# A top-2 mixture of experts layer on one Trainium2 core: residual carried in each expert's rows, last expert added from SBUF

## The chip, the cores and the metric

The program runs on one core of one Trainium2 chip. The metric is the device time of one execution in microseconds (us); lower is better. Engines: PE (TensorE, matrix multiplication), DVE (VectorE), ACT (ScalarE), POOL (GpSimd) and SP (SyncE, which here only issues transfers). SBUF is the on-chip memory of 128 partitions, PSUM holds eight banks of 128x512 floats, into which PE writes.

## The reference

The input is 512 tokens of 1024 floats. A token mixer comes first (input projection, a gated linear recurrence and a short convolution, output projection), then a layer norm. What the change touches is the second half:

```python
alpha = 2 ** 0.25
# h: 512 x 1024, the first norm's output
# 32 experts in 4 groups; each token takes 2 experts of 1 group, with weights w
hid = silu(h @ w_gate[e]) * (h @ w_up[e])          # 1024 -> 256
ffn = sum over the token's 2 experts of w * (hid @ w_down[e])
out = layer_norm(alpha * h + ffn, ln2_g, ln2_b)
```

Each expert has 1 MiB (1,048,576 bytes) each of gate, up and down weights: 96 MiB for 32 experts, read once.

## The kernel before

**Up to the routing (0 to some 187 us).** PE computes the two projections in split float32 while DVE and ACT run the recurrence. Weights of the first experts are loaded as soon as their SBUF is free. Per tile of 128 tokens the first norm's rows `h1` are stored to DRAM (`h1_rows`, two half rows of 2 KB for each token) and the router's logits are taken. Then small matmuls with one-hot operands make two tables, `x_rows` and `y_rows`: for each expert a column of 128 row numbers (64 slots, two half rows each). `x_rows` says where a slot's token lies in `h1_rows`, `y_rows` where the result goes in `y_pairs`, a DRAM buffer of 2 x 512 tokens. Empty slots carry a number outside the buffer and move nothing. Experts with more than 64 tokens get overflow items; with the inputs here there are none.

**The loop over 32 experts.** The work is one list of instructions for each engine, in a fixed order; semaphores tie the lists together. For item q:

- POOL gathers the tokens' rows into `xg` (line 676) and later scatters the results from `ys` (line 681).
- PE, `pe_item`, line 1141: `turn_x(q + 1)` transposes the next item's rows (line 1092), `gate_up(q)` is 16 float32 matmuls (line 1102), `down(q - 1)` is 4 (line 1131), `turn_hid(q)` transposes the hidden values (line 1122). In item 2 there is also a small sum that makes the overflow tables (line 1059).
- DVE copies the transposed rows to SBUF (line 1469), makes `hid` (line 1541), copies it transposed (line 1546). ACT does the silu (line 841) and copies the result out of PSUM to `ys` (line 848).
- SP loads weights into a ring of 8 slots (`RING`). `refill_gu(q)` (line 555) waits for `gu_summed` of item q - 8, `refill_dn(q)` (line 559) for `dn_summed`. Down weights have a ninth slot (`wdn_once`), filled once at 175.96 us, so that those of expert 8 are there without a refill. SP's order is fixed too: a refill that waits holds up those behind it.

There are two row buffers for gathers and two for results (`ROWS = 2`). A gather waits until PE has transposed the buffer's earlier content (line 693), a scatter until ACT has copied the result (line 699).

**The end.** Behind the last weights SP loads `h1` back from DRAM (2 MiB, line 576). The scale and offset of the second norm (`ln2g`, `ln2b`) are asked for once the scatter of expert 28 has landed (line 588). After all scatters SP loads `y_pairs` as eight 512 KB pieces (line 599). PE adds, in PSUM, alpha * h1 by a scaled identity (line 1193) and both experts' rows by diagonal matrices of the routing weights (line 1200); DVE takes the statistics for each of four tiles (line 1585) and finishes the norm with ACT and POOL; SP stores.

Of the kernel before, what the change touches and what calls it, by code (L numbers as in the profile page):

```python
# [21 lines left out]
F32 = mybir.dt.float32  # L22
# [9 lines left out]
P = 128  # L32
# [3 lines left out]
ROWS = 2  # L36
# [11 lines left out]
PIECES = 4  # L48


def hybrid_moe_layer(
# [28 lines left out]
    with ExitStack() as ctx:  # L80
# [15 lines left out]
        ident = sb("ident", [P, P])  # L96
        tri = sb("tri", [P, P], BF16)
        ones = sb("ones", [P, P], BF16)
# [46 lines left out]
        up_block = iota_f[:, 120:120 + 1 + MAX_OVER]  # L145

# [13 lines left out]
        ys = [sb(f"ys{b}", [P, H]) for b in range(ROWS)]  # L160
        xg = [sb(f"xg{b}", [P, H]) for b in (1, 0)][::-1]
# [5 lines left out]
        place[0] = max(place[0], shared + 16384)  # L167
# [15 lines left out]
        wdn.append(at("wdn_once", [P, 2, D], F32, spare + 24576))  # L183
# [52 lines left out]
        iota_i = at("iota_i", [P, 140], I32, y_base + 4096)  # L236
# [7 lines left out]
        h1 = at("h1", [P, TT, D], F32, ring + SLOT)  # L244
        ln2g = at("ln2g", [P, D], F32, ring + SLOT + 16384)
        ln2b = at("ln2b", [P, D], F32, ring + SLOT + 20480)
        pair_y = [[at(f"pair_y{k}_{t}", [P, D], F32, ring + 2 * SLOT + 4096 * (TOP_K * t + k)) for k in range(TOP_K)] for t in range(TT)]


        diag = at("diag", [P, 1 + TOP_K * TT, P], F32, ring + 3 * SLOT + 8192)  # L250
# [6 lines left out]
        hot_slot = at("hot_slot", [P, NP, BLOCK], F16, shared + 4096)  # L257
        hot_x = at("hot_x", [P, NP, N_EXP], F16, shared + 5120)
        hot_y = at("hot_y", [P, NP, N_EXP], F16, shared + 5632)
# [4 lines left out]
        over_slot = at("over_slot", [P, NP, BLOCK], F16, wr_place)  # L264
        over_cmp = at("over_cmp", [1, MAX_OVER, N_EXP], F16, route + 3072)
        assert wr_place + NP * BLOCK * 2 <= wr_place + KT * NR * 4


        DVE_ADDED = 1
# [23 lines left out]
        dn_in = [sem(f"dn_in{s}") for s in range(RING + 1)]  # L293
# [57 lines left out]
        weights_ready = sem("weights_ready")  # L351
# [19 lines left out]
        pairs_in = [[sem(f"pairs_in{t}_{k}") for k in range(TOP_K)] for t in range(TT)]  # L371
        h1_in = sem("h1_in")
        diag_ready = sem("diag_ready")
# [41 lines left out]
        def in_order(rows):  # L415

            return rows.rearrange("p (a m j) -> p m a j", a=2, j=4)
# [28 lines left out]

        def dn_slot_of(q):
            return q if q < RING + 1 else (q - 1) % RING

        def dn_loads_of(q, r):  # L450

            return r + (1 if q < RING + 1 else (q - 1) // RING + 1)
# [42 lines left out]
        def _(sp_):  # L495
# [7 lines left out]

            for q in range(PIECES):
                load_x(q)
                load_first(q)
# [11 lines left out]

            def load_dn(e, s, done):
                sp_.dma_start(wdn[s][:, :, :].rearrange("p j d -> p (j d)"), dn_of(e)).then_inc(done, 16)  # L520
# [27 lines left out]
            load_dn(RING, RING, dn_in[RING])  # L548
# [10 lines left out]
            def refill_dn(q):  # L559
                sp_.wait_ge(dn_summed, q - RING + (0 if q <= 2 * RING else 1))  # L560
                load_dn(q, dn_slot_of(q), dn_in[dn_slot_of(q)])


            for q in range(RING, 2 * RING + 1):
                refill_gu(q)
                if q > RING:
                    refill_dn(q)
            refill_gu(2 * RING + 1)
            for q in range(2 * RING + 1, N_EXP):
                if q + 1 < N_EXP:  # L570
                    refill_gu(q + 1)
                refill_dn(q)

            last_of_1 = max(q for q in range(N_EXP) if slot_of(q) == 1)
            sp_.wait_ge(gu_summed, last_of_1 + 1)
            sp_.dma_start(h1[:, :, :].rearrange("p t (a h) -> p t a h", a=2),
                          h1_rows.rearrange("(t p a) h -> p t a h", p=P, a=2)).then_inc(h1_in, 16)
# [10 lines left out]
            sp_.wait_ge(y_scattered[(N_EXP - 4) % ROWS], 16 * ((N_EXP - 4) // ROWS + 1))  # L588
# [7 lines left out]
            for t in range(TT):  # L596
                for k in range(TOP_K):
                    src = y_pairs[2 * (k * T + t * P):2 * (k * T + (t + 1) * P), :]
                    sp_.dma_start(pair_y[t][k][:, :], src.rearrange("(p a) h -> p (a h)", a=2)).then_inc(pairs_in[t][k], 16)
            for t in range(TT - 1):  # L600

                sp_.wait_ge(out_ready_pool, t + 1)
                sp_.wait_ge(out_ready, t + 1)
                sp_.dma_start(out_rows[t * P:(t + 1) * P, :], pair_y[t][1][:, :]).then_inc(out_stored, 16)
            for h in range(2):

                sp_.wait_ge(out_ready, TT + h)
                cols = slice(h * H, (h + 1) * H)
                sp_.dma_start(out_rows[(TT - 1) * P:, cols], pair_y[TT - 1][1][:, cols]).then_inc(out_stored, 16)
# [4 lines left out]
        def _(pool):  # L614
# [15 lines left out]
            pool.iota(iota_i[:, 108:116], pattern=[[2 * P, TOP_K * TT]], base=-int(NO_ROW), channel_multiplier=2).then_inc(const_pool, 1)  # L630
            pool.memset(iota_i[:, 116:120], int(NO_ROW)).then_inc(const_pool, 1)
            pool.wait_ge(const_pool, 10)
# [3 lines left out]
            pool.wait_ge(const_pool, 11)  # L636
            pool.memset(iota_i[64:128, 116:117], int(NO_ROW) + 1).then_inc(const_pool, 1)
            pool.wait_ge(const_pool, 12)
            pool.memset(zeros[:, :], 0.0).then_inc(const_pool, 1)
            pool.memset(held[:, :], 1.0).then_inc(pool_chain, 1)  # L640
            pool.wait_ge(const_pool, 13)
            pool.tensor_copy(iota_f[:, :], iota_i[:, :]).then_inc(const_done, 1)
# [19 lines left out]
            for t in range(TT):  # L662
                if t == TT - 1:

                    pool.wait_ge(mixed, 2 * TT)
                    for b in range(1, ROWS):
                        pool.memset(xg[b][:, :], 0.0).then_inc(xg_zero, 1)
# [3 lines left out]
            pool.wait_ge(xg_zero, ROWS - 1)  # L671
# [8 lines left out]
            def scatter(b, rows):  # L680
                pool.indirect_dma_start(out=y_pairs, out_offset=bass.IndirectOffsetOnAxis(ap=rows, axis=0),  # L681
                                        in_=ys[b][:, :], in_offset=None,
                                        bounds_check=2 * TOP_K * T - 1, oob_is_err=False).then_inc(y_scattered[b], 16)

            for i in range(1, ROWS):
                gather(i, x_rows[:, i:i + 1])


            SCATTER_LAG = 2
            for i in range(N_EXP + SCATTER_LAG):  # L690
                if i + ROWS < N_EXP:

                    pool.wait_ge(xg_turned, i + 1)
                    gather(i % ROWS, x_rows[:, i + ROWS:i + ROWS + 1])
                done = i - SCATTER_LAG
                if done == 0:
                    pool.wait_ge(rows_ready, 2)
                if done >= 0:
                    pool.wait_ge(y_copied, done + 1)
                    scatter(done % ROWS, y_rows[:, done:done + 1])  # L700

            def over_rows(j):
# [3 lines left out]
                pool.wait_ge(rows_ready, 4)  # L706
# [6 lines left out]
                pool.wait_ge(xg_turned, i)  # L713
# [3 lines left out]
                pool.wait_ge(y_copied, i + 1)  # L717
# [10 lines left out]
            for t in range(TT - 1):  # L728
                z = pair_y[t][1][:, 0:H]
# [7 lines left out]
        def _(act):  # L737
# [105 lines left out]
            def copy_y(i, b, yb, scattered):  # L843
                act.wait_ge(dn_summed, i + 1)

                if not static(scattered) or scattered > 0:
                    act.wait_ge(y_scattered[yb], scattered)
                act.activation(ys[yb][:, :], psum[6 + b][:, :], ACT.Copy).then_inc(y_copied, 1)  # L848

            def copy_main_y(q, r):  # L850
                copy_y(q + r * RING, q % 2, q % ROWS, before(q, r))
# [776 lines left out]
```

## Time and profile before

| | us |
|---|---|
| median of 3 runs | 430.84 (430.11 to 432.84) |
| profiled execution, span from first to last instruction | 432.4 |
| PE busy | 410.6 (95%) |
| DVE busy | 186.8 (43%) |
| ACT busy | 114.5 (26%) |
| POOL busy | 83.1 (19%) |
| bytes moved by DMA | 139.11 MB |

The profiled execution's own time isn't given apart from its span; the longest of the three runs, 432.84, is 0.4 above it. Times inside the trace count from the span's start. A matmul in float32 shows as two records. "DMA share" is the mean busy share of the core's 16 DMA engines, and may come out a little above 1.

### The profile page before, as it was taken

What the parts mean: (1) busy time and instruction counts of PE and PEld (TensorE: products, weight loads), DVE (VectorE), ACT (ScalarE), POOL (GpSimd) and SP (SyncE); (2) the same over time, 40 slices, a digit from 0 to 9 for tenths busy, and PEclk for the clock granted to TensorE, in tenths of its full rate; (3) what the DMA queues carried; (4) which work ended last, traced back from release to release, by engine and by line L of the source; (5) the groups of instructions that cost most, each with busy time, mean ns of one, the idle gap of its engine ahead of it and who ended that gap; (6) DMA issues with size and microseconds to landing.
All of it is one profiled execution on the core that took longest, in us unless ns stands there. A gap on an engine that the chain in (4) does not pass through costs nothing.

```text
span 432.4 us, 6542 instructions
## 1 busy us (share of the span) xinstructions
PE 410.6 (95%) x2578; PEld 277.1 (64%) x2578; DVE 186.8 (43%) x368; ACT 114.5 (26%) x185; POOL 83.1 (19%) x111
## 2 busy tenths in 40 slices
PE   6999999999999999989999999999999999788883
PEld 5888877888888888955555555556555655454331
DVE  1578722499957467855322122212222221111077
ACT  3524376973122002310111111111111111003211
POOL 2201000000000001011332333233223322110124
PEclk8999999999999999998999999999999999898997
DMA  8766340230369999999999999999999999999584
GB/s 266 220 222 208 126 146 28 93 97 31 114 218 420 425 418 420 422 407 378 403 418 413 418 411 412 417 414 411 418 416 417 418 418 416 418 417 416 196 352 194
DMA packets 37377, 139.11 MB, mean 322 GB/s; under 512 B 5107, under 2 KB 17427, under 8 KB 25062
## 3 DMA queue, kind: packets, MB, share of 16 engines
q1 hardware_dynamic: 31184, 126.89, 73.7%
q0 software_dynamic: 6144, 11.84, 7.5%
q8 instruction: 18, 0.29, 0.3%
q10 hardware_dynamic: 22, 0.02, 0.0%
q14 instruction: 9, 0.07, 0.0%
HBM read 134.41 MB, written 12.58 MB: 340 GB/s over the span
## 4 chain that ended last, share of the span: by engine, by line
PE 82%; DMA 11%; DVE 5%; issue 1%; ACT 0%; SPq 0%; DVEq 0%; POOLq 0%
PE bank L1102 24%; PE bank L915 12%; PE bank L917 12%; PE bank L916 12%; PE bank L1131 11%; DMA wgu_first<-in_exp_w_up 7%; PE bank L1092 3%; PE bank L1122 3%; DMA xg<-h_rows,x_rows 2%; DVE stats L1585 1%; DMA pair_y<-y_pairs 1%; PE bank L1012 1%; DMA raw<-in_w_in 1%; PE bank L1024 1%; PE bank L975 1%; PE bank L898 1%
## 5 line engine op out<-in xcount | busy, mean ns | idle before, releaser
L1102 PE MATMUL bank<-wgu,xTg 128*64 128x256 f32 x736 | 87.7, 392 | 3.3 <-DMA wgu<-in_exp_w_up 2.4
L1102 PEld LDWEIGHTS bank<-wgu,xTg 128*64 128x64 f32 x736 | 52.6, 141 | 31.0 <-issue 3.6
L915 PE MATMUL bank<-xT_hi,w_hi 128*128 128x512 f32 x160 | 63.2, 395 | 1.8 <-DVE xT_lo L1242 1.8
L916 PE MATMUL bank<-xT_lo,w_hi 128*128 128x512 f32 x160 | 62.8, 392 | 0.0
L917 PE MATMUL bank<-xT_hi,w_lo 128*128 128x512 f32 x160 | 62.8, 392 | 0.0
L1541 DVE TENSOR_TENSOR hid<-hid,bank 64x256 f32<-64x256 f32 x32 | 13.5, 423 | 105.8 <-ACT hid L841 105.7
L681 POOL DMA_INDIRECT y_pairs<-ys,y_rows x32 | 32.5, 1016 | 134.0 <-PE bank L1092 103.6
L841 ACT ACTIVATE hid<-bank 64x256 f32<-64x256 f32 x32 | 12.1, 377 | 130.8 <-PE bank L1102 130.7
L1131 PE MATMUL bank<-wdn,hidT 128*64 128x512 f32 x192 | 45.3, 593 | 0.0
L1219 DVE TENSOR_TENSOR w_lo<-raw,w_hi 128x2048 fp32r<-128x2048 f32 x12 | 27.5, 2289 | 26.9 <-ACT w_hi L755 26.8
L676 POOL DMA_INDIRECT xg<-h_rows,x_rows x31 | 31.5, 1015 | 31.4 <-issue 19.0
L915 PEld LDWEIGHTS bank<-xT_hi,w_hi 128*128 128x128 f32 x160 | 30.2, 189 | 9.7 <-issue 3.5
L755 ACT ACTIVATE w_hi<-raw 128x2048 fp32r<-128x2048 f32 x12 | 23.0, 1916 | 45.0 <-PE bank L917 37.6
L917 PEld LDWEIGHTS bank<-xT_hi,w_lo 128*128 128x128 f32 x160 | 30.3, 190 | 6.3
L916 PEld LDWEIGHTS bank<-xT_lo,w_hi 128*128 128x128 f32 x160 | 30.2, 189 | 6.0
L848 ACT ACTIVATE ys<-bank 128x512 f32<-128x512 f32 x32 | 19.1, 597 | 46.0 <-PE bank L1131 46.0
L1546 DVE COPY hidT<-bank 128x128 f32<-128x128 f32 x32 | 9.3, 292 | 43.1 <-PE bank L1122 43.1
L1122 PEld LDWEIGHTS bank<-ident,hid 128*128 128x128 f32 x64 | 10.1, 206 | 25.6 <-DVE hid L1541 25.2
L1469 DVE COPY xTg<-bank 128x512 f32<-128x512 f32 x31 | 21.4, 692 | 7.9 <-PE bank L1092 7.9
L1131 PEld LDWEIGHTS bank<-wdn,hidT 128*64 128x64 f32 x192 | 13.7, 137 | 17.0 <-issue 13.8
L1092 PE MATMUL bank<-ident,xg 128*128 128x128 f32 x124 | 20.1, 285 | 1.8 <-DMA xg<-h_rows,x_rows 1.8
L1092 PEld LDWEIGHTS bank<-ident,xg 128*128 128x128 f32 x124 | 17.7, 211 | 1.9 <-DMA xg<-h_rows,x_rows 1.9
(253 smaller groups left out, 497.2 us busy)
## 6 DMA issues: line engine op xcount, KB each, us to landing
wgu<-in_exp_w_gate SPq DMA_DIRECT2D x24, 1024.0 KB, 19.4
wgu<-in_exp_w_up SPq DMA_DIRECT2D x24, 1024.0 KB, 22.4
wdn<-in_exp_w_down SPq DMA_DIRECT2D x24, 1024.0 KB, 22.4
raw<-in_w_in SPq DMA_DIRECT2D x9, 1024.0 KB, 5.2
raw<-in_w_out SPq DMA_DIRECT2D x4, 1024.0 KB, 5.0
wgu_spare<-in_exp_w_gate SPq DMA_DIRECT2D x4, 1024.0 KB, 22.1
wgu_spare<-in_exp_w_up SPq DMA_DIRECT2D x4, 1024.0 KB, 24.3
wdn_first<-in_exp_w_down SPq DMA_DIRECT2D x4, 1024.0 KB, 24.8
```

Source lines behind the costliest of these rows:

```text
L676: pool.indirect_dma_start(out=xg[b][:, :], out_offset=None, in_=h1_rows, in_offset=bass.IndirectOffsetOnAxis(ap=rows, axis=0), bounds_chec ...
L681: pool.indirect_dma_start(out=y_pairs, out_offset=bass.IndirectOffsetOnAxis(ap=rows, axis=0), in_=ys[b][:, :], in_offset=None, bounds_chec ...
L755: act.activation(w_hi[c][:, :], raw[c % 2][:, :], ACT.Copy).then_inc(w_hi_ready, 1)
L915: pe.matmul(dst, a_hi, b_hi, start=start, stop=False)
L916: pe.matmul(dst, a_hi, b_lo, start=False, stop=False)
L917: return pe.matmul(dst, a_lo, b_hi, start=False, stop=stop)
L1092: mm = pe.transpose(psum[b][:, j * P:(j + 1) * P], rows, ident[:, :])
L1102: mm = pe.matmul(psum[2 + b][BLOCK * which:BLOCK * which + BLOCK, 0:F], xTg[b][:, j, h * BLOCK:(h + 1) * BLOCK], wgu[s][:, which, k, :], s ...
L1122: mm = pe.transpose(psum[4 + b][:, j * P:(j + 1) * P], cols, ident[:, :])
L1131: mm = pe.matmul(psum[6 + b][BLOCK * n:BLOCK * n + BLOCK, :], hidT[b][:, j, :], wdn[s][:, j, n * H:(n + 1) * H], start=j == 0, stop=j == 1)
L1219: v.tensor_tensor(w_lo[c][:, :], raw[c % 2][:, :], w_hi[c][:, :], ALU.subtract).then_inc(w_lo_ready, 1)
L1469: v.tensor_copy(xTg[b][:, :, :], psum[b][:, :].rearrange("p (j m) -> p j m", j=4)).then_inc(xTg_ready, 1)
```

## The change

Four things are done together.

1. **Rows.** `ROWS` becomes 8. A result is no longer copied to `ys`: DVE multiplies it by the slot's routing weight and adds it to the gathered row in `xg` (`add_y`), and `xg` itself is scattered. The sum of a token's two rows then holds the residual twice; the weights are scaled by 2/alpha and the norm's epsilon by 4/alpha^2 to suit. For this, item 1 on DVE takes the weights apart into three bfloat16 pieces (`take_weights`, 14 instructions where there were 5) and item 2 on PE sums them into slots (`sum_weights`, 96 small matmuls). ACT has nothing to copy.
2. **Gathers.** Those of experts 1 to 3 are issued at once. Those of 4 to 7 are issued after `rows_ready` has reached 4, that is after the overflow tables of item 2, and after four memsets, since their buffers lie where the routing tables were. A later gather follows the scatter that frees its buffer, six items ahead of its use.
3. **Weights.** `wdn_once` goes; its place is used by four of the row buffers. Expert 8's down weights are an ordinary refill. `down(0)` moves up, ahead of `gate_up(1)`. Expert 31's gate and up weights come in two halves each, behind the down weights of 30, and `gate_up(31)` waits for the second half in its middle. The 2 MiB load of `h1` goes. `ln2g` and `ln2b` are issued right behind the last down weights.
4. **The last expert.** Its gathered rows, without a result, are scattered early. Its result stays in SBUF (`last_y`) and is added by PE through a one-hot matrix (`add_last`). The scatter that the end waits for is that of expert 30. PE adds pairs of rows by `fold` (two identities of 64 on each other) in place of the diagonals.

The diff, cut to its core:

```diff
-ROWS = 2
+ROWS = 8
...
-        wdn.append(at("wdn_once", [P, 2, D], F32, spare + 24576))
+        xg_1, xg_2 = [at(f"xg{b}", [P, H], F32, spare + 28672 + 2048 * n) for n, b in enumerate((1, 2))]
+        xg_4, xg_5 = [at(f"xg{b}", [P, H], F32, spare + 24576 + 2048 * n) for n, b in enumerate((4, 5))]
+        xg = [xg_0, xg_1, xg_2, xg_3, xg_4, xg_5, *xg_route]
...
-            load_dn(RING, RING, dn_in[RING])
...
+            refill_gu(RING)
+            refill_dn(RING)
+            refill_gu(RING + 1)
+            for q in range(RING + 1, N_EXP - 2):
+                refill_gu(q + 1)
                 refill_dn(q)
-            sp_.dma_start(h1[:, :, :].rearrange("p t (a h) -> p t a h", a=2),
-                          h1_rows.rearrange("(t p a) h -> p t a h", p=P, a=2)).then_inc(h1_in, 16)
+            refill_dn(N_EXP - 2)
+            sp_.wait_ge(gu_summed, LAST - RING + 1)
+            for half, done in ((0, gu_in[slot_of(LAST)]), (1, last_gu_in)):
+                ks = slice(half * KT // 2, (half + 1) * KT // 2)
+                for which, w in enumerate((exp_w_gate, exp_w_up)):
+                    src = w[LAST:LAST + 1].rearrange("a (p k) f -> p (a k) f", p=P)[:, ks, :]
+                    sp_.dma_start(wgu[slot_of(LAST)][:, which, ks, :], src).then_inc(done, 16)
+            refill_dn(LAST)
...
-            for i in range(1, ROWS):
+            for i in range(1, 4):
                 gather(i, x_rows[:, i:i + 1])
+            pool.wait_ge(rows_ready, 4)
+            for b in range(4, ROWS):
+                pool.memset(xg[b][:, :], 0.0).then_inc(xg_zero, 1)
+            for b in range(4, ROWS):
+                pool.wait_ge(xg_zero, b)
+                gather(b, x_rows[:, b:b + 1])
+            GATHER_LAG = 2
+            for i in range(N_EXP - 1):
+                if i == LAST - 3:
+                    pool.wait_ge(x_gathered[LAST % ROWS], mains(LAST % ROWS))
+                    scatter(LAST % ROWS, y_rows[:, LAST:LAST + 1])
+                pool.wait_ge(y_copied, i + 1)
+                scatter(i % ROWS, y_rows[:, i:i + 1])
+                done, new = i - GATHER_LAG, i - GATHER_LAG + ROWS
+                if done >= 0 and new < N_EXP:
+                    pool.wait_ge(y_scattered[done % ROWS], 16 * (done // ROWS + 1))
+                    gather(new % ROWS, x_rows[:, new:new + 1])
...
             def pe_item(q, r):
-                if q > 1 and (not static(r) or q + 1 < N_EXP):
+                if q > 2 and (not static(r) or q + 1 < N_EXP):
                     turn_main_x(q + 1, r)
...
+                    turn_hid(0, 0, 2)
                     turn_main_x(1, 0)
+                    main_down(0, 0)
                     return
                 gate_up(q + r * RING, slot_of(q), q % 2, 2, loads_of(q, r))
...
                 if q == 2:
+                    turn_main_x(3, 0)
                     pe.wait_ge(over_hot_ready, 2)
                     sum_rows(3, 0, over_slot, over_x_hot)
-                    sum_rows(3, MAX_OVER, over_slot, over_y_hot).then_inc(over_summed, 1)
+                    sum_rows(3, MAX_OVER, over_slot, over_y_hot)
+                    pe.wait_ge(hot_w_ready, 2)
+                    sum_weights(3, 2 * MAX_OVER, hot_slot_b, hot_w)
+                    sum_weights(3, 2 * MAX_OVER + N_EXP, over_slot_b, over_w).then_inc(over_summed, 1)
...
+            def add_y(i, g, b):
+                v.wait_ge(dn_summed, i + 1)
+                col = slot_weight[:, i:i + 1] if static(i) else slot_weight[:, bass.ds(i, 1)]
+                v.scalar_tensor_tensor(out=xg[g][:, :], in0=psum[6 + b][:, :], scalar=col, in1=xg[g][:, :],
+                                       op0=ALU.mult, op1=ALU.add).then_inc(y_copied, 1)
...
+            add_pairs(0)
+            add_pairs(1)
+            pe.wait_ge(last_y_copied, 1)
+            add_last(0, 0)
+            add_last(1, 0)
+            add_last(0, 1)
+            add_last(1, 1)
+            for t in range(2, TT):
+                add_pairs(t)
+                add_last(t, 0)
+                add_last(t, 1)
```

`take_over` on DVE, in item 2, waits for `over_summed` and gives `rows_ready` its third and fourth count. `add_pairs(t)` is four matmuls on the two pieces of tile t, each into 64 partitions; `add_last(t, turn)` is two, with 64 contraction rows and 256 columns.

## Rows read from the trace of the kernel before

**Rows 1.** Page, part 2: DMA engines' share and GB/s, 40 slices of 10.8 us

```profile
DMA  8766340230369999999999999999999999999584
GB/s 266 220 222 208 126 146 28 93 97 31 114 218 420 425 418 420 422 407 378 403 418 413 418 411 412 417 414 411 418 416 417 418 418 416 418 417 416 196 352 194
```

**Rows 2.** Windows: busy us by engine, then granted PE clock, DMA share, GB/s

```profile
201.00:202.00 1.00, 1.00 (x10) 0.85 (x10) 0.31 (x2) 0.38 (x1) 0.00 (x0) 1.00 0.53 197
202.00:203.00 1.00, 1.00 (x6) 0.48 (x8) 0.97 (x2) 0.00 (x0) 0.29 (x1) 1.00 0.74 209
...
300.00:390.00 90.00, 86.02 (x626) 49.15 (x624) 18.31 (x40) 13.04 (x27) 25.81 (x26) 0.98 1.02 417
390.00:399.00 9.00, 6.98 (x42) 3.66 (x40) 0.69 (x2) 3.15 (x11) 0.99 (x1) 0.81 1.01 416
```

**Rows 3.** Timeline of SP: start us, us, the transfer issued

```profile
201.05 0.33 SPq L516 DMA_DIRECT2D wgu<-in_exp_w_gate  x1
...
215.21 0.33 SPq L516 DMA_DIRECT2D wgu<-in_exp_w_gate  x1
...
370.59 2.68 SPq L520 DMA_DIRECT2D wdn_first<-in_exp_w_down  x1
```

**Rows 4.** The chain that ended last, first items: start us, us, what

```profile
187.18 7.00 DMA xg<-h_rows,x_rows
...
195.85 5.17 PE bank L1102 x32
...
208.39 0.48 PE bank L1059 x32
...
211.56 3.60 PE bank L1102 x32
...
217.80 3.60 PE bank L1102 x32
```

**Rows 5.** Tile xg: its memset (ns) and its gathers' time to landing

```profile
L667 POOL MEMSET xg<- x1: 525/525/525, 170.9 to 170.9; 128x512 f32 x1
...
DMA to landing us min/median/max: 6.5/7.0/8.3
```

**Rows 6.** Transfers issued from 212 to 400 us: queue of the indirect ones, counts

```profile
q0 software_dynamic: 4404, 7.23, 10.3%
...
y_pairs<-ys,y_rows POOLq DMA_INDIRECT x29, 6.7
xg<-h_rows,x_rows POOLq DMA_INDIRECT x26, 7.1
```

**Rows 7.** Transfers issued at 370 to 374 us: KB each, us to landing

```profile
wdn_first<-in_exp_w_down SPq DMA_DIRECT2D x1, 1024.0 KB, 28.7
...
h<-h_rows SPq DMA_DIRECT2D x1, 2048.0 KB, 31.0
```

**Rows 8.** The chain that ended last, the end

```profile
393.69 5.24 PE bank L1102 x32
...
401.51 1.95 PE bank L1131 x8
...
404.85 3.38 DMA y_pairs<-ys,y_rows
408.29 0.33 SPq L599
...
415.15 1.31 DVE stats L1585 x2
```

**Rows 9.** Tile y_pairs: its scatters' time to landing

```profile
DMA to landing us min/median/max: 3.4/6.6/9.2
```

**Rows 10.** Timeline of the end: start us, us, instruction, idle before it

```profile
404.44 7.10 PE L1193 MATMUL bank<-h,diag 128*128 128x512 f32 x16 [0.99 <-DMA h<-h_rows]
...
413.62 1.50 DVE L1580 SCALAR_TENSOR_TENSOR bank<-pair_y,weight,bank 128x512 f32<-128x512 f32 x2 [12.21 <-DMA pair_y<-y_pairs]
...
414.93 10.57 PE L1200 MATMUL bank<-pair_y,diag 128*128 128x512 f32 x24 [0.60 <-DMA pair_y<-y_pairs]
```

More of the change, by code:

```diff
@@ L48 @@
 PIECES = 4
+PARTS = 3
+HOT = 2.0 ** -7
+LAST = 31
 def hybrid_moe_layer(
@@ L1061, in sum_rows, with sum_weights @@
                 return mm
+            def sum_weights(bank, col, slots, hots):
+                for n in range(NP):
+                    for half in range(2):
+                        for c in range(PARTS):
+                            mm = pe.matmul(psum[bank][half * BLOCK:(half + 1) * BLOCK, col:col + hots.shape[3]], slots[:, n, :], hots[:, c, n, :],
+                                           start=n == 0 and c == 0, stop=n == NP - 1 and c == PARTS - 1)
+                return mm
             def take_first(n, tiles):
@@ L1093, in turn_x, with gate_up @@
                 mm.then_inc(xg_turned, 1)
-            def gate_up(i, s, b, lag, loads):
+            def gate_up(i, s, b, lag, loads, late=None):
                 pe.wait_ge(gu_in[s], 32 * loads)
@@ L1100, in gate_up @@
                     h, j = divmod(k, 4)
+                    if late is not None and k == KT // 2:
+                        pe.wait_ge(late, 32)
                     for which in range(2):
@@ L1180, in pe_over @@
                 turn_hid(i, 0, 1)
-                down(i, 0, 0, 1, loads)
+                down(i, 0, 0, 2, loads)
             overflow(pe, pe_over)
             n = pe.value_load(n_over[0:1, 0:1], min_val=0, max_val=MAX_OVER)
-            pe.wait_ge(y_copied, n + N_EXP)
-            pe.wait_ge(h1_in, 16)
-            pe.wait_ge(diag_ready, 1)
-            for t in range(TT):
-                for h in range(2):
-                    pe.matmul(psum[2 * t + h][:, :], diag[:, 0, :], in_order(h1[:, t, :])[:, h * H // 8:(h + 1) * H // 8], start=True, stop=False)
@@ L1194, in _ @@
[L1194 to L1203 removed]
+            pe.wait_ge(y_copied, n + N_EXP - 1)
@@ new lines, in _, with add_pairs, add_last @@
+            pe.wait_ge(fold_ready, 1)
+            def add_pairs(t):
+                for u in (2 * t, 2 * t + 1):
+                    pe.wait_ge(pairs_in[u], 16)
+                for h in range(2):
+                    for q in range(2):
+                        pe.matmul(z_of(t, h)[BLOCK * q:BLOCK * (q + 1), :], fold[:, :], in_order(pair_y[2 * t + q][:, :], h), start=True, stop=False)
+            def add_last(t, turn):
+                if turn == 1:
+                    pe.wait_ge(last_half_added, 2 * t + 2)
+                for h in range(2):
+                    a = h ^ turn
+                    rows = slice(BLOCK * a, BLOCK * (a + 1))
+                    pe.matmul(part_of(z_of(t, h), a), last_hotT[rows, t, :], last_y[rows, h * F:(h + 1) * F],
+                              start=False, stop=turn == 1).then_inc(z_summed if turn else last_half_added, 1)
@@ L1575, in _ @@
             for t in range(TT):
-                if t < DVE_ADDED:
-                    v.wait_ge(pairs_in[t][1], 16)
-                    for h in range(2):
-                        v.wait_ge(z_summed, 2 * t + h + 1)
-                        step(v.scalar_tensor_tensor(out=z_of(t, h), in0=pair_y[t][1][:, h * H:(h + 1) * H], scalar=weight[:, 1, t:t + 1], in1=z_of(t, h),
-                                                    op0=ALU.mult, op1=ALU.add))
-                    v.wait_ge(dve, chain[0])
                 for h in range(2):
```

252 lines of the change are left out of this document (137 added, 115 removed).

## The prediction

> **What bounds the kernel now.** I read the slices first, then the chain, then windows and the issues of SP. PE is busy 95% of the span, and the chain puts most of it on PE, so PE looks like the bound. The slices of the DMA engines say otherwise for the second half [rows 1]: from slice 13 (130 us) to slice 37 (400 us) their share is 9 tenths or more, at 378 to 425 GB/s. Window by window they are never idle between 300 and 399 us, at 416 to 417 GB/s [rows 2]; PE, in the same 90 us, has 4 us without work. So from 130 to 400 us the engines that move bytes are the limit, and what counts is how many bytes must be moved before the last weights are there, and for how long the DMA engines have nothing to do meanwhile. In the trace of before that is a short time only: in 201 to 203 us the shares are 0.53 and 0.74, together 0.73 us dry [rows 2]. There the weights issued so far had run out, and the next ones were issued at 201.05, when PE had finished item 1 [rows 3]. The reader should keep this: a refill waits for PE, PE is ahead by a ring of 8 slots at most, and the ring is at its limit just in these first items. Later SP's backlog is some 28 us [rows 7], and a stall of PE costs nothing.
>
> The last down weights are issued at 370.59 and land 28.7 later, at 399.3 [rows 3, 7]. From there to the end of the span (432.4) are 33.1 us. I call 399.3 W; the time is W plus this tail, and I work out what the change does to each. The sums stand against the span of 432.4. The median of the runs shown is 430.84, 0.4% below, and I carry the difference over as a ratio.
>
> **Bytes before W.** The 2 MiB of h1 go, but they were issued behind the last weights and landed at 373.3 + 31.0 = 404.3 [rows 7]: nothing gained in W. The ninth down slot was 1 MiB loaded early; the same MiB now comes a little later: no change in the sum, but the DMA engines have 2.5 us (1.05 MB at 0.417 MB per us, rows 2) less to do before 201.5. `down(0)` moves up and frees its slot by about 197 to 198.5, so expert 8's down weights come about as the others run out. I put the dry time of this stretch at 0.7 as before; bounds are 0 and 2 us, since the order down(0), gate_up(1) can shift the issue of 201.05 by about 1 us either way. Two more scatters lie before W than before (31's, which is early, and 29's or 30's). One indirect transfer moves 7.23 MB / 55 = 0.13 MB [rows 6], or 0.3 us at that rate: W + 0.6.
>
> **Item 3, where I see the price.** Gather 4 used to be issued in the run of things. Now it waits for rows_ready at 4, so for the sums in item 2, and PE's first instruction in item 3 is the transpose of its rows. PE works in order, so `gate_up(3)`, whose own operands are ready, waits behind it. Worked out from the end of gate_up(2), which is where line 1059 starts, 208.4 [rows 4]. DVE's longer take_weights lies beside gate_up(1): its two wide products have 768 and 384 columns, so 1.1 and 0.6 at the 0.75 for 512 columns of rows 10, and a dozen small steps bring it to about 4 us, an estimate; gate_up(1) took 5.2 [rows 4]. I let 208.4 stand, with 1 us either way. Then:
>
> - transpose of item 3's rows 0.5, the overflow sums 0.5 as now (32 matmuls in 0.48, rows 4);
> - sum_weights, 96 matmuls of that kind: 96 x 0.015 = 1.4 by that row; the same with some spacing 2.4; I take 2.0;
> - take_over on DVE and the handing over to POOL: 0.6;
> - four memsets of 128x512: 4 x 0.525 = 2.1 [rows 5];
> - gather 4, from issue to landing: 7.0 [rows 5], with 6.5 and 8.3 as ends under load; a transfer of this kind on an empty queue took 3.4 [rows 9], which is the lower bound;
> - transpose 0.5, then gate_up(3). After a PE idle time of 2 us or so it has run at the lower clock level: 5.17 and 5.24 instead of 3.60 [rows 4, 8]. PE will have been idle for about 7 us, so 5.2; bounds 3.6 and 5.2.
>
> Sum: 208.4 + 0.5 + 0.5 + 2.0 + 0.6 + 2.1 + 7.0 + 0.5 + 5.2 = 226.8 for the end of gate_up(3), where it was 215.2 [rows 3]. That alone would be harmless. But the gate and up weights of expert 11 are issued only then, and everything of SP stands behind them.
>
> What can the DMA engines do until then? At 201.5 they had run dry with 27 MiB of expert weights delivered (0 to 8). Until gate_up(3) ends, the ring allows gate and up weights of 0 to 10 and down weights of 0 to 9: 32 MiB. The 5 MiB take 5.24 / 0.417 = 12.6 us; gathers 4 to 7 and two scatters take 6 x 0.31 = 1.9. They are done at 201.5 + 14.5 = 216.0 at the latest supply. The next bytes flow about 1.2 us after the issue (as at 201.05: issue, and full again at about 202.5), at 228.0. That is 12.0 us dry, against 0.7 before: W + 11.3. With gather 3.4, gate_up 3.6 and sums 1.4 it would be 11.3 - 3.6 - 1.6 - 0.6 = 5.5; with gather 8.3 and the other dry times on top 13.5. The loss isn't made good later: the share is 1.0 already from 210 on [rows 1], at a steady rate, and PE is not the bound even then. It would reach the end of gate_up(31) at 226.8 + 28 x 6.24 = 401.5 (6.24 is the time from gate_up(3) to gate_up(4), 211.56 to 217.80, rows 4), while its weights land at about 408.7.
>
> The Trainium skill, DMA: Bandwidth & Descriptors, section "Anatomy of one DMA — SWDGE (gpsimd) path", gives a transfer issued from GpSimd about 2.0 us plus bytes over 436 GB/s, which for 0.13 MB is 2.3 us, an estimate by that page. No gather of the trace comes near it (6.5 at least, beside full queues). By that page the dry time would be 4.7 us less and the sum below 4.7 us lower; the trace's figure is the one used.
>
> **The loop after that.** DVE takes over the copy out of PSUM as a scalar_tensor_tensor of 128x512, 1.50 / 2 = 0.75 us [rows 10], in an item of 6.24 us of which it is busy a fifth (18.31 of 90, rows 2): nothing; turn_hid follows make_hid as before and the new add stands behind it. Down weights are read with 16-byte runs; h1 was so read in the matmuls of line 1193, which took 7.10 / 16 = 0.44 each, as those with plain rows, 10.57 / 24 = 0.44 [rows 10]: nothing. Gathers are six items ahead: nothing. POOL's extra constants at the start run while the first loads are under way: nothing. If this cover were gone, an item could grow by 0.75 us at most, and the ring's backlog would take it.
>
> **The tail.** With w for the new W: gate and up weights of 31 now land behind the down weights of 30, their second half at w - 2.5. At that time PE has done the first half or is in it, and down(30). gate_up's second half ends at about w - 0.2, silu, product, transpose and copy take 1.9, down(31) 1.7 to 1.95 [rows 8]: the result is there at w + 3.5, where down(31) ended at W + 4.2 (403.5). It no longer has to go through DRAM. The scatter of 30 follows down(30) (end about w - 4.3) and the add (0.75): issued at w - 3.4, landed at about w + 2.5 (6.6 under load, 3.4 quiet, rows 9; the queue goes quiet within it). It was W + 9.0 (408.29). Then eight pieces are loaded as before. The third one landed at 414.9, 6.6 after the first issue [rows 8, 10], the fourth about 1.3 later, 7.9. PE's new order wants four pieces before tile 0 is complete: add_pairs(1) ends 1.7 after the fourth (four half-width matmuls, as line 1131's), and three add_last another 0.9 to 1.7. So the statistics of tile 0 begin at w + 2.6 + 7.9 + 1.7 + 1.3 = w + 13.5; they began at W + 15.9 (415.15, rows 8). From there it is DVE's work as before, four tiles and the last store, 17.3 us. ln2g and ln2b are there by then either way (nothing gained). The tail is 30.8, against 33.1: gain 2.3, with 1 and 5.6 as bounds (the latter if scatter 30 lands at w).
>
> **Sum.** 432.4 + 11.3 + 0.6 - 2.3 = 442.0 in the profile, 2.2% more. On the median: 430.84 x 442.0 / 432.4 = 440.4; I say 440.
>
> **Rivals.**
>
> A, *the stall of item 3 is covered* (the other side). Mechanism: gather 4 lands, or the DMA engines have work in hand, until gate_up(3) ends; the tail's gain stands alone. For it: PE stalls late in the loop cost nothing. It decides at one point, whether the 5 MiB allowed by the ring last until the next issue; for that gate_up(3) would have to end by 215, 12 us earlier than my sum. Time: 432.4 + 0.6 - 2.3 = 430.7, in the median 429; with the best tail (5.6) 425.8 on the median, faster by 1.2%. Against it: the order of PE's and POOL's lists leaves no way round. Chance 0.13, of which 0.05 for over 1% faster.
>
> B, *half the stall*: the quiet gather (3.4), full clock and quick sums: dry time 5.5. Time 432.4 + 5.5 + 0.6 - 2.3 = 436.2, median 434.6. For it: the queue does go quiet at 216, while gather 4 is on its way (issued at 214). Chance 0.2, half of it within 1%.
>
> C, *the tail gains nothing or loses*: add_pairs(1) ahead of tile 0 and a scatter that takes 9.2 under load make the tail 33.1 again: 444.3, median 442.7. Chance 0.17.
>
> **How the numbers follow.** My forecast has 0.5, B 0.2, C 0.17, A 0.13. A measurement of this kernel can tell about 1% from no change. Slower by over 1% (above 435.1): 0.5 + 0.17 + 0.1 = 0.77. Within 1%: half of B and 0.08 of A, 0.18. Faster by over 1%: 0.05. The range is from between A and B, 433, to above C, 444.
>
> **What would show it.** In the profile after: in the windows from 200 to 232 us a stretch of 5 us or more with a DMA share near 0, just ahead of SP's issue for expert 11 at about 227; PE idle for about 7 us ahead of the transpose of item 3, released by the gather; gathers 4 to 7 issued at about 214; from there on the same 6.24 us items as before, 11 us late; late PE waits for weights as now; the last down weights landing at about 411; the first pair load issued less than 4 us behind them; and 17 us from the first statistics of tile 0 to the end. The prediction is wrong if PE meets gather 4 ready or the share stays at 1, or if the tail from the last weights to the end is far from 31 us.

## The result and the profile after

| | before | after |
|---|---|---|
| median of the runs, us | 430.65 (430.11 to 432.84, 4 runs) | 442.82 (441.69 to 444.02, 4 runs) |
| span of the profiled execution, us | 432.4 | 442.1 |
| time of the profiled execution, us | not given | 443.94 |
| PE busy, us | 410.6 | 409.0 |
| DVE busy, us | 186.8 | 207.5 |
| ACT busy, us | 114.5 | 94.0 |
| bytes moved by DMA | 139.11 MB | 137.03 MB |

The ratio after to before is 1.027, 95% interval 1.023 to 1.031: slower. The forecast was 440 with a range from 433 to 444.

First the slices of the changed kernel, 11.05 us each, which answer to [rows 1]. The first slice counts as 1.

```profile
DMA  8766532022379999998849999999999999999734
GB/s 264 235 200 198 180 105 78 19 95 96 95 286 424 423 417 427 394 375 340 338 167 416 413 416 413 412 416 413 415 416 416 419 416 416 419 416 401 265 152 190
```

Slice 21 (221 to 232 us) is the hole: 167 GB/s, where every other slice of the expert loop up to the last three moves 338 or more. From slice 22 to slice 36 the rate is 412 to 419, as it was before (411 to 418), so what is lost in the hole is never made up. Now window by window, with the columns of [rows 2].

```profile
206.00:208.00 2.00, 2.00 (x16) 1.15 (x12) 0.00 (x0) 0.00 (x0) 0.00 (x0) 0.63 0.83 344
208.00:210.00 2.00, 2.00 (x72) 1.59 (x70) 0.69 (x1) 0.38 (x1) 0.00 (x0) 1.00 0.32 61
...
214.00:216.00 2.00, 0.00 (x0) 0.00 (x0) 0.00 (x0) 0.00 (x0) 1.70 (x2) 1.00 1.02 381
...
220.00:222.00 2.00, 1.77 (x8) 1.25 (x10) 0.60 (x1) 0.00 (x0) 0.99 (x1) 0.50 0.31 113
222.00:224.00 2.00, 2.00 (x12) 1.05 (x12) 0.09 (x1) 0.00 (x0) 0.00 (x0) 0.50 0.14 49
224.00:226.00 2.00, 2.00 (x20) 1.26 (x18) 0.00 (x0) 0.00 (x0) 0.00 (x0) 0.86 0.00 0
226.00:228.00 2.00, 2.00 (x14) 0.66 (x10) 0.42 (x1) 0.38 (x1) 0.00 (x0) 1.00 0.24 41
```

Two engines are idle one after the other. PE has nothing from 214 to 220 us while the DMA engines still work; they run dry when PE works again. Taking 1 minus the share of each microsecond (where the share is under 0.9), the dry time from 190 to 232 us is 9.4 us; before it was 0.7. There is a second, smaller hole three microseconds ahead of that count. The first of these rows is from the kernel before, the other two are from the changed one:

```profile
187.00:188.00 1.00, 1.00 (x9) 0.63 (x10) 0.42 (x1) 0.00 (x0) 0.82 (x1) 1.00 1.01 410
...
187.00:188.00 1.00, 1.00 (x12) 0.62 (x10) 0.36 (x2) 0.00 (x0) 0.84 (x1) 1.00 0.39 147
188.00:189.00 1.00, 1.00 (x10) 0.47 (x6) 0.23 (x1) 0.00 (x0) 0.86 (x1) 1.00 0.56 131
```

That is 1.05 us dry. SP issued no weights between 175.17 and 187.85 us. The kernel before had issued one MiB more, for the ninth down slot, and kept the engines busy with it until the next weights came. From 232 to 395 us no microsecond has a share under 0.9, in either kernel.

The instructions around the large hole (timeline of the changed kernel):

```profile
203.00 5.36 PE L1121 MATMUL bank<-wgu,xTg 128*64 128x256 f32 x32
...
208.40 0.33 SPq L538 DMA_DIRECT2D wgu<-in_exp_w_gate  x1
...
209.50 0.91 PE L1076 MATMUL bank<-hot_w,hot_slot 128*64 128x32 bf16 x48
...
210.26 0.91 PE L1076 MATMUL bank<-over_w,over_slot 128*64 128x16 bf16 x48
...
211.66 1.92 POOL L715 MEMSET xg<- 128x512 f32 x4 [21.18 <-DVE y_rows L1580]
...
213.74 1.01 POOL L702 DMA_INDIRECT xg<-h_rows,x_rows  x1 [0.15 <-POOL xg L715]
...
220.23 1.13 PE L1109 MATMUL bank<-ident,xg 128*128 128x128 f32 x4 [6.71 <-DMA xg<-h_rows,x_rows]
...
221.29 5.27 PE L1121 MATMUL bank<-wgu,xTg 128*64 128x256 f32 x32
...
226.60 0.33 SPq L538 DMA_DIRECT2D wgu<-in_exp_w_gate  x1
```

Read from below: expert 11's weights are issued at 226.60, when gate_up(3) has ended; gate_up(3) starts at 221.29, behind the transpose, which waited 6.71 us for gather 4 (issued 213.74, landed 6.5 later); the gather waited for the memsets, and these for DVE's overflow tables, behind the sums. Between the issues of experts 10 and 11 lie 18.2 us (208.40 to 226.60). Before, they lay 6.8 apart (215.21 in [rows 3], against the 208.4 of [rows 4]).

The end, first SP's timeline and the landing of the last down weights:

```profile
385.00 2.13 SPq L524 DMA_DIRECT2D wdn_extra<-in_exp_w_down  x1
...
411.78 4.35 SPq L618 DMA_DIRECT2D pair_y<-y_pairs  x8
```

```profile
wdn_extra<-in_exp_w_down SPq DMA_DIRECT2D x1, 1024.0 KB, 24.1
```

The last down weights land at 385.0 + 24.1 = 409.1 (before 399.3, [rows 3, 7]), and from there to the end are 33.0 us (before 33.1). Both parts differ from the forecast, 411.2 and 30.8. The chain of the end shows why the tail gained nothing:

```profile
405.75 5.88 DMA y_pairs<-xg,y_rows
...
412.16 4.26 DMA pair_y<-y_pairs
416.42 0.14 issue
416.56 3.68 PE bank L1231 x8
...
420.24 3.05 PE bank L1231 x8
423.29 1.55 PE bank L1241 x12
...
424.85 0.04 issue
424.89 1.31 DVE stats L1680 x2
```

The first piece is asked for 2.7 us behind the last weights, as forecast (2.6). But the statistics of tile 0 begin 13.1 us later, not 10.9: the two add_pairs took 3.68 and 3.05 us, with PE at its lower level, as this window says:

```profile
420.00:421.00 1.00, 1.00 (x4) 0.32 (x4) 0.00 (x0) 0.00 (x0) 0.00 (x0) 0.50 1.03 414
```

The granted clock is 0.50 (1.2 of 2.4 GHz) from 416 to 422 us, after PE had had nothing to do for 4.3 us.

### The profile page after: what moved, and what is told of

Same layout as the page of the kernel before. It is cut to its first block, busy times and chain, and to the rows that moved or that the text cites. A ratio compares the mean times of both kernels' runs of the same rounds, so it can differ in the third digit from the quotient of the medians.

```text
span 442.1 us, 6782 instructions
## 1 busy us (share of the span) xinstructions
PE 409.0 (93%) x2698; PEld 276.2 (62%) x2698; DVE 207.5 (47%) x410; ACT 94.0 (21%) x146; POOL 86.2 (20%) x119
## 2 busy tenths in 40 slices
DMA packets 37139, 137.03 MB, mean 310 GB/s; under 512 B 5124, under 2 KB 17444, under 8 KB 25079
## 4 chain that ended last, share of the span: by engine, by line
PE 79%; DMA 13%; DVE 5%; issue 1%; SPq 1%; ACT 0%; POOL 0%; DVEq 0%; POOLq 0%
PE bank L1121 21%; PE bank L923 11%; PE bank L925 11%; PE bank L924 11%; PE bank L1150 9%; DMA wgu_spare<-in_exp_w_up 7%; PE bank L1109 3%; PE bank L1141 2%; DMA raw<-in_w_in 2%; PE bank L1231 2%; DMA xg<-h_rows,x_rows 1%; DMA y_pairs<-xg,y_rows 1%; DVE stats L1680 1%; PE bank L1020 1%; PE bank L906 1%
## 5 line engine op out<-in xcount | busy, mean ns | idle before, releaser
L1121 PE MATMUL bank<-wgu,xTg 128*64 128x256 f32 x736 | 89.4, 398 | 2.2 <-DMA wgu<-in_exp_w_up 2.1
L1121 PEld LDWEIGHTS bank<-wgu,xTg 128*64 128x64 f32 x736 | 53.7, 143 | 31.2 <-issue 4.9
L1622 DVE TENSOR_TENSOR hid<-hid,bank 64x256 f32<-64x256 f32 x32 | 13.5, 423 | 101.9 <-ACT hid L872 101.8
L707 POOL DMA_INDIRECT y_pairs<-xg,y_rows x32 | 32.1, 1003 | 123.9 <-DVE xg L1632 123.0
L1632 DVE SCALAR_TENSOR_TENSOR xg<-bank,slot_weight,xg 128x512 f32<-128x512 f32 x31 | 23.3, 751 | 28.0 <-PE bank L1150 28.0
L1141 PE MATMUL bank<-ident,hid 128*128 128x128 f32 x64 | 16.2, 334 | 4.5 <-DVE hid L1622 4.4
```

The source lines that it names most:

```text
L1121: mm = pe.matmul(psum[2 + b][BLOCK * which:BLOCK * which + BLOCK, 0:F], xTg[b][:, j, h * BLOCK:(h + 1) * BLOCK], wgu[s][:, which, k, :], s ...
L1141: mm = pe.transpose(psum[4 + b][:, j * P:(j + 1) * P], cols, ident[:, :])
L1632: v.scalar_tensor_tensor(out=xg[g][:, :], in0=psum[6 + b][:, :], scalar=col, in1=xg[g][:, :], op0=ALU.mult, op1=ALU.add).then_inc(y_copied, 1)
```

## The experiments

Two theories stood against each other at the outset. *Theory*: the loss is the time in which the DMA engines have nothing to do because gate_up(3) is late, and it is late for gather 4. *Rival*: the loss lies elsewhere, in DVE's added work for each item or in the end, and a stall of PE is absorbed. All ratios are to the kernel before, run on the same chip.

To compare runs I use two numbers besides the ratio. W is when the last down weights land (issue plus time to landing), and the rate in one window from 200 to 236 us says how many bytes went through the stretch in dispute. This is its row for the kernel before:

```profile
200.00:236.00 36.00, 36.00 (x290) 20.69 (x287) 11.21 (x29) 5.60 (x12) 11.21 (x11) 1.00 0.99 400
```

and for the changed kernel:

```profile
200.00:236.00 36.00, 26.64 (x278) 15.79 (x280) 10.67 (x23) 1.13 (x3) 9.97 (x12) 0.86 0.74 291
```

(400 - 291) x 36 / 416 = 9.4 us worth of bytes are missing, at the steady rate of 416; W is 9.8 us later.

The traces differ by up to 1.7 us before the loop begins. So I also count W from a common mark, SP's issue of expert 7's gate weights, up to which the variants of one kernel are the same: 188.26 before, 187.85 in the changed kernel. From there W comes after 211.0 us before and after 221.2 with the change, 10.2 later.

### The sums one item earlier

```diff
                 if q == 1:
                     turn_main_x(2, 0)
+                    pe.wait_ge(over_hot_ready, 2)
+                    pe.wait_ge(hot_w_ready, 2)
+                    sum_rows(7, 0, over_slot, over_x_hot)
+                    sum_rows(7, MAX_OVER, over_slot, over_y_hot)
+                    sum_weights(7, 2 * MAX_OVER, hot_slot_b, hot_w)
+                    sum_weights(7, 2 * MAX_OVER + N_EXP, over_slot_b, over_w).then_inc(over_summed, 1)
                     turn_hid(1, 1, 2)
                     return
```

The same sums go out of item 2, and take_over and take_slot_weights on DVE move to item 1, behind make_hid.

> The changed kernel with the four sums (overflow tables and slot weights) in item 1 of PE, into another bank, instead of item 2, and take_over on DVE there too. Theory (the loss is the time in which the DMA engines are dry because gate_up(3) waits for gather 4): gather 4 is issued at about 206.4 instead of 213.7, gate_up(3) ends at 218 to 219 instead of 226.4, the dry time between 206 and 230 us falls from 9.5 to about 2, and the span from 442.1 to about 435 (ratio to the kernel before 1.010). Rival (the loss lies in the tail or in DVE's added work in each item): 442 still.

Ratio 1.006 (1.003 to 1.009), median 434.35, span 433.3. Its timeline and its window:

```profile
205.48 1.00 POOL L702 DMA_INDIRECT xg<-h_rows,x_rows  x1 [0.16 <-POOL xg L715]
...
211.53 0.65 PE L1109 MATMUL bank<-ident,xg 128*128 128x128 f32 x4
...
215.82 0.33 SPq L538 DMA_DIRECT2D wgu<-in_exp_w_gate  x1
```

```profile
200.00:236.00 36.00, 35.24 (x358) 20.72 (x358) 12.39 (x28) 1.88 (x5) 14.05 (x16) 0.95 0.95 382
```

The transpose at 211.53 has no wait in front of it: gather 4, issued 8.3 us earlier than in the changed kernel, is there. W is 400.1, 9.0 earlier. From the common mark (186.97) it comes after 213.1 us, 2.1 later than before instead of 10.2. All the rest of the change is still in, DVE's adds and the new end among it. The ratio gives back 2.1 of the 2.7 per cent. So some eight tenths of the loss hang on this wait, and the rival falls for that part. What remains, 0.6% (0.3 to 0.9), lies in W too: the dry time is 2.2 us from 190 to 232 and another 1.0 ahead of 190, against 0.7 and nothing before. It moved more than expected (433.3 against 435, gate_up(3) ended at 215.8 instead of 218 to 219), since PE in item 3 didn't wait at all.

### The late gather alone, in the kernel before

```diff
                     pool.wait_ge(xg_turned, i + 1)
+                    if i == 2:
+                        pool.wait_ge(rows_ready, 4)
+                        for n in range(4):
+                            pool.memset(xg[0][:, :], 0.0).then_inc(xg_zero, 1)
+                            pool.wait_ge(xg_zero, ROWS + n)
                     gather(i % ROWS, x_rows[:, i + ROWS:i + ROWS + 1])
```

> The kernel before with one thing of the change put in: its gather 4 waits for rows_ready at 4 and for four memsets of 128x512. Theory: gate_up(3) ends at about 224 instead of 215.2, the DMA engines are dry for some 7 to 8 us that they were not, since the ring then allows 6 MiB more (it has the ninth down slot), and the span goes from 432.4 to about 439 (ratio 1.016). Rival (a stall of PE this early is absorbed, as those late in the loop are): ratio 1.000.

Ratio 1.016 (1.013 to 1.020), median 438.89. Timeline and window:

```profile
217.34 1.13 PE L1097 MATMUL bank<-ident,xg 128*128 128x128 f32 x4 [8.31 <-DMA xg<-h_rows,x_rows]
...
218.40 4.82 PE L1107 MATMUL bank<-wgu,xTg 128*64 128x256 f32 x32
...
223.26 0.33 SPq L516 DMA_DIRECT2D wgu<-in_exp_w_gate  x1
```

```profile
200.00:236.00 36.00, 27.68 (x220) 15.79 (x221) 9.02 (x24) 3.77 (x8) 11.26 (x13) 0.91 0.83 327
```

The cause put in by hand makes the same picture: PE waits 8.31 us for the gather, expert 11's weights are issued at 223.26, and (400 - 327) x 36 / 416 = 6.3 us of bytes are missing. This is the second leg: without the rest of the change, the wait alone makes the kernel slower by the 1.6% expected. The dry time expected, 7 to 8 us, came out smaller, 6.0 by the shares, and the span is 437.1 instead of 439. W itself is 403.0, only 3.7 later than in the profile of before, but this execution was ahead of that one before anything had been changed: its first gather was issued at 185.65 instead of 187.18, its gate_up(1) began at 193.81 instead of 195.85 [rows 4]. From the common mark (186.75) W is 5.2 later, and the end behind it is 1.0 longer.

### gate_up(3) ahead of the transpose

```diff
-                if q > 2 and (not static(r) or q + 1 < N_EXP):
+                if q > 2 and q != 3 and (not static(r) or q + 1 < N_EXP):
                     turn_main_x(q + 1, r)
...
+                if q == 3:
+                    turn_main_x(4, r)
                 main_down(q - 1, r)
```

> The changed kernel with gate_up(3) ahead of the transpose of item 4's rows on PE, in this item alone. Theory: the weights of expert 11 are issued at about 217 instead of 226.6, but gate_up(4) still waits for gather 4 and ends at about 227; the ring allows 2 to 3 MiB more meanwhile, so the dry time falls from 9.5 to about 5 and the span by about 4 (ratio 1.016). Rival (the loss lies elsewhere): 1.027 still.

Ratio 1.017 (1.012 to 1.021), median 438.56, W 402.5.

```profile
215.09 0.33 SPq L538 DMA_DIRECT2D wgu<-in_exp_w_gate  x1
...
218.16 1.13 PE L1109 MATMUL bank<-ident,xg 128*128 128x128 f32 x4 [3.12 <-DMA xg<-h_rows,x_rows]
...
226.91 0.33 SPq L538 DMA_DIRECT2D wgu<-in_exp_w_gate  x1
```

```profile
200.00:236.00 36.00, 30.62 (x322) 17.83 (x324) 12.01 (x27) 1.50 (x4) 12.02 (x14) 0.95 0.96 367
```

As expected, the long distance between issues moved to the next expert (215.09 to 226.91), and about half of the loss went: four tenths by the ratio, six tenths by W from the common mark, in the fastest of its four executions. The expectation of 5 us dry was wrong in an instructive way: the shares add up to 1.4 us only, but the bytes of the window are 2.9 us short, and W is 3.2 late. From 216 to 222 us, with gathers and scatters under way, the shares are 0.91 to 1.09 at 301 to 387 GB/s. So such transfers keep the engines busy at a lower rate; bytes are the better measure.

### Tile 0 first

```diff
-            add_pairs(0)
-            add_pairs(1)
-            pe.wait_ge(last_y_copied, 1)
-            add_last(0, 0)
-            add_last(1, 0)
-            add_last(0, 1)
-            add_last(1, 1)
-            for t in range(2, TT):
+            for t in range(TT):
                 add_pairs(t)
+                if t == 0:
+                    pe.wait_ge(last_y_copied, 1)
                 add_last(t, 0)
                 add_last(t, 1)
```

> The changed kernel with tile 0 completed ahead of add_pairs(1) at the end. Theory (the tail gained nothing because tile 0 waits for four pieces): the statistics of tile 0 begin about 3 us earlier after the last weights, tile 1 then waits 1 us, the span falls by 2 to 3 (ratio 1.021). Rival (the end is set by the lower clock of PE and the landing of the pieces alone): within 0.5 us.

Ratio 1.018 (1.014 to 1.023), median 439.42. W is 406.8, the span 437.1, so the end is 30.3 us long instead of 33.0. PE's timeline:

```profile
413.96 3.68 PE L1231 MATMUL bank<-pair_y,fold 128*64 128x512 f32 x8 [4.05 <-DMA pair_y<-y_pairs]
417.57 2.31 PE L1241 MATMUL bank<-last_y,last_hotT 64*128 64x256 f32 x8
419.81 1.94 PE L1231 MATMUL bank<-pair_y,fold 128*64 128x512 f32 x8
```

add_last(0) follows add_pairs(0) directly, and the statistics of tile 0 begin 2.6 us earlier after W, near the 3 expected. The 2.7 us are the price of asking for four pieces before tile 0. The ratio moved further than that alone would (0.009, some 3.7 us), and its interval ends just where that of the changed kernel begins; W too was 2.3 earlier in this profile, which the edit doesn't touch (1.3 of it lies ahead of the common mark, 186.56).

### PE kept busy ahead of the end

```diff
             pe.wait_ge(fold_ready, 1)
+            keep_busy(psum[0], 34)
```

> The changed kernel with 34 transposes of the identity on PE while it waits for the first pieces at the end; nothing of the result changes. Theory (part of the tail is PE's lower clock: add_pairs took 3.7 and 3.1 us instead of 1.7): add_pairs(0) takes 1.7 us, add_pairs(1) waits for the fourth piece (at about 8.5 us behind the first issue), the statistics of tile 0 begin about 2 us earlier and the ratio to the kernel before is 1.022 instead of 1.027. Rival (the landing of the fourth piece sets the time): under 0.5 us, 1.026.

Ratio 1.024 (1.021 to 1.029), median 443.26, W 410.2, end 32.0.

```profile
413.48 3.90 PE L906 MATMUL bank<-ident 128*128 128x128 f32 x34 [0.17 <-issue]
417.44 1.94 PE L1232 MATMUL bank<-pair_y,fold 128*64 128x512 f32 x8
421.51 1.94 PE L1232 MATMUL bank<-pair_y,fold 128*64 128x512 f32 x8 [2.14 <-DMA pair_y<-y_pairs]
```

The clock stays up and add_pairs takes 1.9, but PE then waits 2.14 us for the fourth piece: the end is 1.0 shorter, not 2. The ratio lies between the two expectations, and its interval holds both; the median isn't below that of the changed kernel. By the trace the clock is a part of it, and the pieces' landing takes back half of what it gave.

### All three, and a warm PE in item 1

> The changed kernel with three repairs: the sums in item 1, tile 0 completed first, PE kept busy ahead of the end. Theory (stall and tail are separate, so the gains add): 434.4 less 3.3 us, since tile 1 then waits for its pieces; ratio 0.998. Rival (once PE is warm the order doesn't matter, or the pieces' landing sets the rest): ratio 1.003.

The edits are those above together. Ratio 1.000 (0.998 to 1.003), median 431.9, W 400.1, end 30.1. The interval holds both expectations, 0.998 and 1.003. By the traces the repairs add up: 3.1 us less in the span than with the sums alone, all of it in the end. Counted from the first load of a piece to the end of the span, the changed kernel takes 30.3 us, 29.6 with the sums alone, 27.7 with tile 0 first, 29.3 with PE kept busy and 26.5 with everything.

The last kernel has two edits more: 14 transposes in item 1, and each of the gathers 4 to 7 issued behind its own memset.

```diff
                     turn_main_x(2, 0)
+                    keep_busy(psum[4], 14)
                     pe.wait_ge(over_hot_ready, 2)
...
                 pool.memset(xg[b][:, :], 0.0).then_inc(xg_zero, 1)
-            for b in range(4, ROWS):
                 pool.wait_ge(xg_zero, b)
```

> The same with 14 transposes of the identity on PE in item 1 while it waits for DVE's products, and gather 4 issued behind its own memset instead of behind all four. Theory (the dry time left is the late issue of expert 10's weights, because gate_up(2) ran at the lower clock): gate_up(2) takes 3.6 instead of 5.2 us, the dry time falls from 2.2 to about 0.7, ratio 0.995. Rival (the DMA engines run dry there anyway, for want of the ninth down slot): ratio as without it.

Ratio 0.998 (0.996 to 1.000), median 430.38 against 431.71 for the kernel before, W 399.6, end 28.7. Its window, and the issue for expert 10:

```profile
200.00:236.00 36.00, 35.86 (x376) 21.71 (x376) 13.71 (x31) 1.88 (x5) 14.27 (x16) 1.00 0.98 392
```

```profile
207.18 0.33 SPq L538 DMA_DIRECT2D wgu<-in_exp_w_gate  x1
```

The granted clock over the window is 1.00 instead of 0.95, gate_up(2) takes 3.67 us instead of 5.25, expert 10's weights are issued at 207.18 instead of 208.66, and the dry time is 0.9 us, against 1.9 without these two edits and 0.7 in the kernel before. The earlier issue is the clock's; how the rest divides between the two edits was not tried. The ratio moved by about half of what was expected (0.995).

In this stretch the ninth down slot isn't missed. It is missed earlier: around 187 us all seven kernels without it are dry for 1.0 to 1.3 us, and the two that have it (the one before, and its copy with the late gather) not at all. It is a part of why the gain is only 1.3 us in the medians though the end is 4.4 shorter than before (28.7 against 33.1): W from the common mark (187.14) still comes 1.5 later. That the slot alone would bring this back was not tried. This kernel is the fastest of those built, by 0.2%, at the edge of what was measured.

## Why the prediction was right, and where it wasn't

**The bound.** That bytes per time set the length from 130 to 400 us, and not the engine that is 95% busy, is shown by the traces: no microsecond from 232 to 395 has a share under 0.9, at the same 416 GB/s before and after, and PE still waits for weights near the end. These are its waits from 240 us on, in the changed kernel:

```profile
PE bank L1121 <- DMA wgu<-in_exp_w_up: 2.1, 1, 2.1
PE bank L1121 <- DMA wgu_spare<-in_exp_w_up: 0.2, 1, 0.2
```

In the kernel before they are 5.9 us. The two cross-checks show what the late gather costs (take it out, and W comes back by 9.0 us; put it into the kernel before, and that kernel is 1.6% slower), but by themselves they would fit a loop bound by PE as well.

**Item 3.** gate_up(3) ends at 226.6; the forecast was 226.8. Term by term: end of gate_up(2) 208.3 (208.4), though by another way than assumed, a start 1.7 us sooner and the lower clock; sum_weights 1.5 (2.0); memsets 1.9 (2.1); gather 4 6.5 (7.0); gate_up(3) 5.3 (5.2). Of the signs named, the idle PE (6.7 us), the gathers at 214 and the shift of what follows by 11 us were seen; the share was 0.00 from 223 to 227 us only, and under 0.3 from 221.

**Dry time: the mis-sized term.** Forecast 12.0 against 0.7 before, measured 9.4 against 0.7: 8.7 instead of 11.3. The end of the stretch is right (the next bytes flow at about 228). The beginning isn't: the engines had work until about 219, not 216.0. The step that failed is "At 201.5 they had run dry with 27 MiB of expert weights delivered". In the changed kernel the share was still 1 then and stayed there until 207 us:

```profile
201.50:228.00 26.50, 18.64 (x220) 10.93 (x220) 5.73 (x14) 0.75 (x2) 7.95 (x10) 0.81 0.66 251
```

In this stretch 6.65 MB moved (251 GB/s for 26.5 us), where the forecast has 5.24 for weights and 0.79 for six indirect transfers: 0.6 MB, or 1.5 us, had been left over. And the engines were busy for 17.5 us (a share of 0.66), where 6.65 MB at 0.417 take 15.9, so the bytes were also 1.5 us slower than the steady rate, as the third experiment shows for indirect transfers. Some 0.4 MB of what was left over is what the hole at 187 to 189 us cost (1.05 us at 0.417 MB per us, an estimate). The forecast had put the loss of the ninth slot at nothing ("no change in the sum"). The weights of expert 10 came into a queue already empty (206 to 210 us, 1.7 us dry); that moves a part of the dry time forward and doesn't change its sum. With the 1.05 the dry time is 9.7 more than before, and W is 9.8 later, so nothing of size is left for "two more scatters, 0.6", which was not measured apart.

**The tail: the other mis-sized term, of the other sign.** Forecast a gain of 2.3, measured 0.1. The scatter of 30 and the first load came as forecast. What failed is the step from the first load to the statistics of tile 0, which was 7.9 to the fourth piece, 1.7 for add_pairs(1) and 1.3 for add_last: 10.9 us in the forecast, 13.1 measured. I had weighed the lower clock for gate_up(3) but not for the end, where PE idles 4.3 us. That is only a part of it. With the clock up (experiment five) the step still takes 12.2: the fourth piece is there 8.65 after the first load, not 7.9, add_pairs(1) takes 1.9 and add_last 1.6. The order is the larger price, 2.7 with tile 0 first (experiment four); it was in the forecast.

**The sum.** 442.0 forecast for the span and 442.1 measured is luck to the extent of 2.1 us late in one term and 2.2 early in the other. On the median the forecast was 440.4, or 440, and 442.8 came. That step was wrong as well: it set the span of 432.4 against the median of the runs as if they belonged together. The profiled execution of the changed kernel gives 443.94 for a span of 442.1, 1.8 us. In the 36 later executions of the kernel before the same difference is 1.7 to 1.8. So its profile of 432.4 belongs to an execution of about 434.2, well above its median, and the median stands for a span near 428.8, an estimate. The profile was one of the longer executions, and the loss in medians (12.2) is larger than in profiles (9.7). Two bounds don't come out of their own terms either, and nothing rested on them: 13.5 for the dry time (11.3 and 1.3 for the gather and 1.3 for the other dry time make 13.9), and 5.6 for the tail's gain (2.3 and 2.5 for the scatter make 4.8).

**The rivals.** A, the covered stall: fallen, the issue came 11 us after the one of before. B, half the stall: gather 4 took 6.5 us though the queue was emptying, and the clock was low; fallen. C: true for the tail's size and for the order that it names, not for the scatter of 9.2, which took 5.9; its span of 444.3 is 2.2 too long, so its 442.7 for the median is near 442.8 by luck. The estimate by the Trainium skill, DMA: Bandwidth & Descriptors, section "Anatomy of one DMA — SWDGE (gpsimd) path", 2.3 us for such a gather, isn't borne out: 6.5 from issue to landing in this trace too.

**The other parts.** DVE's adds (31 of 751 ns) cost nothing in the loop, as forecast: from 240 to 390 us the rate is 415 GB/s, as before (416). That h1's 2 MiB and ln2g and ln2b bring nothing fits W and the tail, but was not tried alone.

## What to carry to other kernels

When a loop is bound by transfers through a ring, look at the first items, where the ring is at its limit: a wait of one engine that a backlog would cover later leaves the DMA engines without work there, and that is never made up. Before an operand is prepared later than it was, ask which instruction stands behind its consumer in the same engine's order, and what that one would have released. And size the end with the clock that an idle PE will have, not with the one of the busy loop.

## What the runs showed of the hardware that was not expected

- In the changed kernel PE had no work for 2.6 us (200.0 to 202.6). Behind it the granted clock was 0.50 to 0.54 from 204 to 207 us, and gate_up(2) took 5.36 us instead of 3.6. Fourteen transposes of the identity in that gap kept the granted clock at 1.00 in the last kernel, and gate_up(2) took 3.67.
- The share of the DMA engines can stay near 1 while the bytes fall short: from 200 to 236 us 0.96 at 367 GB/s in the third experiment, with the four gathers and the scatters close together, 0.99 at 400 before.
- Executions of the same instructions differ by 1.5 us before the expert loop begins: the gather of expert 1 was issued at 187.18 us in the profile of the kernel before, and at 185.65 in its copy with the late gather, which is the same up to there. What makes the difference was not looked into.
